# Fourteen modulation blocks: split fp32r products exchanged for plain fp32 products on four column groups

## What is computed

```python
mod = (jax.nn.silu(c) @ w_ada + b_ada)[:, None, :]
sh1, sc1, gt1, sh2, sc2, gt2 = jnp.split(mod, 6, axis=-1)
h = rmsnorm(x, g_mix) * (1 + sc1) + sh1
z = h @ w_in
...
x = x + gt1 * (merged @ w_out)
h2 = rmsnorm(x, g_ffn) * (1 + sc2) + sh2
```

## Time and profile before

| | |
|---|---|
| median of 3 runs | 1964.58 us (1964.14 to 1965.5) |
| profiled execution | 1967.0 us, of which the span from first to last instruction is 1965.3 us |
| TensorE busy | 1908.4 us (97%) |
| weight loads busy | 1815.0 us (92%), beside the matmuls |
| VectorE, ScalarE, GpSimd busy | 829.4 us (42%), 621.2 us (32%), 128.4 us (7%) |
| DMA | 257.70 MB, mean 131 GB/s |

### The profile page before, as it was taken

One profiled execution on the slowest core, in us unless ns is written; L12 is line 12 of the kernel. 1 busy time (PEld: TensorE's weight loads), 2 busy tenths in 40 slices (PEclk: granted clock), 3 DMA queues, 4 the chain that ended last, 5 costly groups with the idle time before them and its releaser, 6 DMA issues.

```text
span 1965.3 us, 30471 instructions
## 1 busy us (share of the span) xinstructions
PE 1908.4 (97%) x12193; PEld 1815.0 (92%) x12193; DVE 829.4 (42%) x1363; ACT 621.2 (32%) x952; POOL 128.4 (7%) x245
## 2 busy tenths in 40 slices
PE   7999999999999999999999997899999999999998
PEld 4799989999999997777899997899999999999998
DVE  5422222213334333232553558844455545564542
ACT  4331222222434433121210215533333334343432
POOL 0010009201000002221000000000000000000000
PEclk9999999999999999999999998999999999999999
DMA  8653434452343345544642350422232223774641
GB/s 273 239 177 120 132 122 135 140 151 73 93 128 106 92 150 129 165 142 143 203 123 89 90 175 25 109 67 67 71 111 80 65 65 119 261 240 149 214 152 63
DMA packets 254045, 257.70 MB, mean 131 GB/s; under 512 B 15476, under 2 KB 213160, under 8 KB 253952
## 3 DMA queue, kind: packets, MB, share of 16 engines
q1 hardware_dynamic: 244830, 222.81, 37.7%
q10 hardware_dynamic: 7721, 29.25, 3.7%
q0 software_dynamic: 1408, 4.46, 0.8%
HBM read 189.97 MB, written 66.63 MB: 131 GB/s over the span
## 4 chain that ended last, share of the span: by engine, by line
PE 92%; DVE 3%; ACT 2%; DMA 1%; issue 1%; SPq 0%; ACTq 0%; DVEq 0%
PE dense L2340 44%; PE dense L2760 17%; PE dense L2805 10%; PE misc L2760 5%; PE misc L2805 3%; PE misc L2641 2%; PE misc L2628 1%; PE misc L2567 1%; PE misc L2571 1%; PE misc L2540 1%; DMA ada_w<-in_w_ada_dram 1%; PE dense L2414 1%; PE misc L2569 1%; PE misc L2461 1%; PE misc L2460 1%
## 5 line engine op out<-in xcount | busy, mean ns | idle before, releaser
L2340 PE MATMUL dense<-act_hi,w_hi 128*128 128x384 f32 x1704 | 401.2, 343 | 5.8 <-DVE act_lo L1593 3.0
L2340 PE MATMUL dense<-act_lo,w_hi 128*128 128x384 f32 x1704 | 377.4, 329 | 0.0
L2340 PE MATMUL dense<-act_hi,w_lo 128*128 128x384 f32 x1704 | 376.9, 329 | 0.0
L2340 PEld LDWEIGHTS dense<-act_hi,w_hi 128*128 128x128 f32 x1704 | 291.9, 189 | 28.3 <-issue 21.4
L2340 PEld LDWEIGHTS dense<-act_hi,w_lo 128*128 128x128 f32 x1704 | 293.0, 189 | 0.0
L2340 PEld LDWEIGHTS dense<-act_lo,w_hi 128*128 128x128 f32 x1704 | 292.0, 189 | 0.0
L1588 DVE TENSOR_TENSOR w_lo<-raw,w_hi 128x1024 fp32r<-128x1024 f32 x73 | 92.4, 1267 | 265.9 <-ACT w_hi L1028 265.8
L1124 ACT ACTIVATE stage<-dense 128x768 f32<-128x768 f32 x52 | 42.2, 812 | 285.1 <-PE dense L2340 285.0
L1028 ACT ACTIVATE w_hi<-raw 128x1024 fp32r<-128x1024 f32 x73 | 77.3, 1060 | 167.7 <-PE dense L2340 167.3
L2047 DVE TENSOR_TENSOR w_lo<-hmT,w_hi 128x512 fp32r<-128x512 f32 x120 | 78.9, 686 | 101.2 <-ACT w_hi L1334 101.2
L1334 ACT ACTIVATE w_hi<-hmT 128x512 fp32r<-128x512 f32 x120 | 72.6, 623 | 81.2 <-PE dense L2760 80.8
(11 more groups left out here) (435 smaller groups left out, 3051.2 us busy)
## 6 DMA issues: line engine op xcount, KB each, us to landing
z_scratch<-stage ACTq DMA_DIRECT2D x52, 544.0 KB, 2.7
raw<-in_w_in_dram SPq DMA_DIRECT2D x53, 512.0 KB, 3.8
ada_w<-in_w_ada_dram SPq DMA_DIRECT2D x24, 1024.0 KB, 5.5
hmT<-in_w_gate_up_dram SPq DMA_DIRECT2D x40, 512.0 KB, 6.1
raw<-in_w_down_dram SPq DMA_DIRECT2D x34, 512.0 KB, 4.4
stage<-in_w_down_dram SPq DMA_DIRECT2D x32, 512.0 KB, 4.4
stage<-z_scratch SPq DMA_DIRECT2D x24, 544.0 KB, 3.7
a_scratch<-sums SPq DMA_DIRECT2D x34, 272.0 KB, 4.8
```

The source lines that it names most:

```text
L2340: ins = pe.matmul(tile(k, c), w[:, n % 2, off:off + P], x[:, xr, t0:t1], start=(first and p == 0), stop=(last and p == 2))
```

## The change

The late blocks are made as plain fp32 products. There are no high and low parts of the late `w_ada` blocks and of the condition any more; `c32` holds the condition in 32 columns (9 used, the rest zero). The 8 tiles of the contraction go in turn to four column groups of the array, each with 32 columns, so that each group adds up two tiles, and the four partial sums stand in PSUM rows 0, 32, 64 and 96 on. ScalarE copies all 128 rows. The turn is a product with a 0/1 matrix `pick` (128 x 9), which adds the four partial sums while it turns them. GpSimd makes `pick` from the identity. VectorE then has one operation per block. The blocks go into two slots of `ada_w` in turn, and a load waits until the modulation of the block two before is written (`mod_ready`).

```diff
         c32 = sb(halved, "c32", [P, KT, CW])
-                if per or j:
-                    sp.wait_ge(ada_cut, i * per + j)
+                if per or j > 1:
+                    sp.wait_ge(mod_ready, i * per + j - 1)
                 else:
-                    sp.wait_ge(mrow_ready, 7)
-                sp.dma_start(ada_w[:, 0, :, :], w_cols(...)
+                    sp.wait_ge(mrow_ready, (7, 10)[j])
+                sp.dma_start(ada_w[:, j % 2, :, :], w_cols(...)
...
+            pool.wait_ge(consts_ready, 3)
+            link(pool.tensor_tensor(pick[:, :], ident[:, 0:GRP], ident[:, CW:CW + GRP], ALU.add))
+            for j in range(2, P // CW):
+                link(pool.tensor_tensor(pick[:, :], pick[:, :], ident[:, CW * j:CW * j + GRP], ALU.add))
...
-            def ada_high(j, i=0):
-                act.activation(wa_hi[:, :, :], ada_w[:, 0, :, :], ACT.Copy).then_inc(adahi_ready, 1)
-            act.activation(c_hl[:, :, 0:GRP], cT[:, :, :], ACT.Copy).then_inc(chi_ready, 1)
-            ada_high(0)
+            act.activation(c32[:, :, 0:GRP], cT[:, :, :], ACT.Copy).then_inc(chi_ready, 1)
...
-                        act.activation(ada_rows[:, :], bank(r, 256, 2 * GRP), ACT.Copy).then_inc(round_free[r % 2], 1)
-                        if not last or j == 0:
-                            ada_high(1 + j // 2, i)
+                        act.activation(ada_rows[:, :], bank(r, 256), ACT.Copy).then_inc(round_free[r % 2], 1)
...
-                dve.tensor_tensor(wa_lo[:, :, :], ada_w[:, 0, :, :], wa_hi[:, :, :].bitcast(F32), ALU.subtract
-                                  ).then_inc(ada_cut, 1)
+            dve.memset(c32[:, :, GRP:CW], 0.0).then_inc(c_ready, 1)
...
-                    for col in range(2):
-                        ...
-                        ins = dve.tensor_scalar(out, t[:, 0:GRP], vec[:, ds(m + V_ADA, 1)], None, ALU.add)
-                        ...
-                        ins = dve.tensor_tensor(out, out, t[:, GRP:2 * GRP], ALU.add)
+                    dve.tensor_tensor(mod[:, ds(m, 2), :], bank(r, 2 * GRP).rearrange("p (m g) -> p m g", g=GRP),
+                                      vec[:, ds(m + V_ADA, 2)].unsqueeze(2).to_broadcast([P, 2, GRP]), ALU.add
+                                      ).then_inc(mod_ready, 1)
+                    dve.wait_ge(mod_ready, i + 1)
                     dve.sem_inc(round_free[r % 2], 1)
...
-                pe.wait_ge(ada_cut, i * (per // 2) + (jt // 2 + 1))
+                pe.wait_ge(ada_in[jt // 2], i * (per // 4 * 16) + 16)
-                for kk in range(KT):
-                    pe.matmul(bank(r, 256, 2 * GRP), c_hl[:, kk, :], wa_hi[:, kk, :], start=(kk == 0), stop=False)
-                    ins = pe.matmul(bank(r, 256, GRP), c_hl[:, kk, 0:GRP], wa_lo[:, kk, :], start=False,
-                                    stop=(kk == KT - 1))
+                for k0 in (0, KH):
+                    for j in range(KH):
+                        ins = pe.matmul(bank(r, 256)[CW * j:CW * j + CW, :], c32[:, k0 + j, :], ada_w[:, jt // 2, k0 + j, :],
+                                        start=(k0 == 0), stop=(k0 == KH))
...
-                    ins = pe.transpose(misc[:, r % 2, 2 * GRP * col:2 * GRP * (col + 1)],
-                                       ada_rows[:, P * col:P * col + P], ident[0:2 * GRP, 0:2 * GRP])
+                    ins = pe.matmul(misc[:, r % 2, GRP * col:GRP * col + GRP], ada_rows[:, P * col:P * col + P], pick[:, :],
+                                    start=True, stop=True)
...
                     pe.wait_ge(c_ready, 1)
+                    pe.wait_ge(consts_ready, 4)
```

More of the change, by code:

```diff
@@ L80 @@
 ADA0 = 20
+CW = 32
 ADA_EARLY = (0, 4, 1, 5, 2, 6, 3, 7, 8, 9)
@@ L130, in trunk @@
         epsc = sb(top, "epsc", [P, 1])
+        pick = sb(top, "pick", [P, GRP])
         raw = sb(top, "raw", [P, 2, 1024])
@@ L163, in trunk @@
         sb(halved, "over_x", [P, TT * D + KT * T + 600])
[L164 to L168, removed]
+        sb(halved, "over_ada_w2", [P, 2048])
+        c32 = sb(halved, "c32", [P, KT, CW])
+        ada_rows = sb(halved, "ada_rows", [P, 256])
         halved.close()
@@ L544, in late_ada_load @@
                 a = ADA0 // 2 + j
-                if per or j:
-                    sp.wait_ge(ada_cut, i * per + j)
-                else:
-                    sp.wait_ge(mrow_ready, 7)
-                sp.dma_start(ada_w[:, 0, :, :], w_cols(w_ada[0], i * (256 * per) + 256 * a, 256)
+                if per or j > 1:
+                    sp.wait_ge(mod_ready, i * per + j - 1)
+                else:
+                    sp.wait_ge(mrow_ready, (7, 10)[j])
+                sp.dma_start(ada_w[:, j % 2, :, :], w_cols(w_ada[0], i * (256 * per) + 256 * a, 256)
                              ).then_inc(ada_in[a % 2], 16)
@@ L1028, in split_hi @@
                 act.activation(w_hi[:, n % 2, :], raw[:, n % 2, :], ACT.Copy).then_inc(hi_ready, 1)
-            def ada_high(j, i=0):
-                wait_full(act, ada_in, j, i, 2, 16)
-                act.activation(wa_hi[:, :, :], ada_w[:, 0, :, :], ACT.Copy).then_inc(adahi_ready, 1)
             act.dma_start(cc[0:1, :], c_prompt).then_inc(c_in, 16)
@@ L1676, in _ @@
                 early_mod(e)
-            def ada_low(j, i=0):
-                dve.wait_ge(adahi_ready, i + (j + 1))
-                dve.tensor_tensor(wa_lo[:, :, :], ada_w[:, 0, :, :], wa_hi[:, :, :].bitcast(F32), ALU.subtract
-                                  ).then_inc(ada_cut, 1)
             dve.wait_ge(chi_ready, 1)
-            dve.tensor_tensor(c_hl[:, :, GRP:2 * GRP], cT[:, :, :], c_hl[:, :, 0:GRP].bitcast(F32), ALU.subtract
-                              ).then_inc(c_ready, 1)
-            ada_low(0)
+            dve.memset(c32[:, :, GRP:CW], 0.0).then_inc(c_ready, 1)
             split_lo(2)
@@ L1697, in body @@
                     if not last:
-                        ada_low(1, i)
                         split_lo(U_L1 + 3, i, 2)
                     wait_full(dve, round_full, r, i, 2)
-                    for col in range(2):
[L1702 to L1705, removed]
-                        ins = dve.tensor_scalar(out, t[:, 0:GRP], vec[:, ds(m + V_ADA, 1)], None, ALU.add)
-                        ins.then_inc(mod_ready, 1)
-                        dve.wait_ge(mod_ready, i * 4 + (2 * col + 1))
-                        ins = dve.tensor_tensor(out, out, t[:, GRP:2 * GRP], ALU.add)
-                        ins.then_inc(mod_ready, 1)
-                        dve.wait_ge(mod_ready, i * 4 + (2 * col + 2))
+                    m = i * 2 + ADA0
+                    dve.tensor_tensor(mod[:, ds(m, 2), :], bank(r, 2 * GRP).rearrange("p (m g) -> p m g", g=GRP),
+                                      vec[:, ds(m + V_ADA, 2)].unsqueeze(2).to_broadcast([P, 2, GRP]), ALU.add
+                                      ).then_inc(mod_ready, 1)
+                    dve.wait_ge(mod_ready, i + 1)
                     dve.sem_inc(round_free[r % 2], 1)
```

## The result

The changed kernel takes 1954.71 us (median of 5 runs, 1953.17 to 1955.3), the kernel before 1965.5 us beside it (5 runs, 1964.14 to 1966.55): a ratio of 0.9944, 95% interval 0.9929 to 0.9958, so 10.8 us or 0.6% less. The forecast was 1969.4, slower; what came is rival 1 (1954.2). The stated range, 1953 to 1972, holds the result only because it reached over both cases. The profiled execution took 1953.43 us, its span is 1951.7 us.

What follows compares the result with a forecast made beforehand. TensorE's own queue was taken as the bound: per late block 2.26 - 1.88 + 0.01 = +0.39 us, +5.5 over 14 blocks, less 0.7 for one wait, +4.8. Forecast 1969.4 us, slower, range 1953 to 1972.

Steps and rivals of the forecast that it cites:

- rival 1: Late blocks' products: four column groups run side by side, -0.69 us per block, 1954.2 us in all; chance 0.30, partly so included.
- 9 steps: Late product: one group's second half runs with the next group's first, nothing passes; 2.26 us against 1.88, chance 0.48.
- The bound: Late blocks, 88 to 456 us: TensorE's queue counts; removing VectorE's and ScalarE's parts, some 59 us, gains only at one wait.
- The changes of shape: Around each late product, array going narrow and back: 0.09 + 0.03 + 0.09 + 0.11 = 0.32 us per block.
- The step: Late product: instructions on the same columns start 0.2154 us apart, as read from the early blocks.
- The turn: After each late product: two full products in two halves each, 0.44 us against 0.43, +0.01 per block.
- The wait: TensorE before the pooling rows' transposes: 4.03 us shortens to 3.3, a gain of 0.7, kept at 0 to 2.3.
- The clock: After the pooling-row wait, granted at 0.57 over 4 us; a shorter gap escaping that might give up to 1.6 us more.
- The own range: Whole kernel if the likeliest case holds, varying 0.1 less or 0.15 more per block and the clock: 1966.4 to 1971.9 us.
- The moved loads: Late loads wait for an earlier modulation; a weight load moves from 304.59 to about 315 us, 5 us of cover left.
- The three prices: Late product at 16, 9 or 4 steps: 3.77, 2.26 or 1.18 us, against 1.88 before.
- 4-step case: Late product with four groups always side by side: 1.18 us against 1.88, 1954.2 us in all; chance 0.30, partly so included.

Runs made afterwards that it cites:

- The first experiment: Changed kernel with a late block's eight matmuls ordered by groups 0, 0, 1, 1, 2, 2, 3, 3 instead of 0, 1, 2, 3 twice: 1955.13 us, ratio 0.9948.
- How far ahead: Changed kernel with the late product issued group by group, each group's two matmuls made four times over: 2102.01 us, ratio 1.0689 to the kernel before.
- the double product: Changed kernel with the whole product of each late block made twice in a row: 1965.58 us, ratio 0.9999 to the kernel before.
- the cheap early products: Changed kernel with the ten early modulation blocks also made on four column groups and turned by the 0/1 product: 1948.64 us, ratio 0.9908 to the kernel before.

## Why the prediction was wrong

**The step that failed** is the choice of 9 steps: "if groups can run side by side but no matmul passes an earlier one (in all rows here matmuls start in program order)". The premise was read from rows in which every matmul uses the same columns as the one before, and there a column that is busy and an order that is kept look alike: the earlier trace rows could not tell them apart. I said so of the groups ("no row has two neighbours in the queue on different groups") but not of the order, which rests on the same rows. The first experiment shows halves starting past as many as nine earlier ones, and the experiment "How far ahead" that this goes as far as four halves of each group. The Trainium skill, page TensorE: Matmul & The Clock Gate (Part 3, The mechanism), says that matmuls are strictly first in, first out; the trace does not agree for fp32 matmuls on different column groups, and the measurement decides. With the rule of the Trainium skill's page TensorEngine Tiling (Key Properties), that tiles operate independently, the trace agrees: 16, 8 and 4 steps on one, two and four groups. It agrees only as far as no group has more than two matmuls in line, as the experiment "How far ahead" shows.

That one term is 14 x (2.26 - 1.19) = 15.0 us, and the forecast and the result lie 14.7 us apart. The rest of the sum, point by point:
- **The bound.** Right: 39 us of VectorE's and 20 us of ScalarE's work fell away in the stretch of the late blocks, and TensorE's rhythm moved by TensorE's own part alone.
- **The changes of shape**, 0.32 us per visit, put together from the column sums: 0.33 by the double product, which takes them as one. By the raw starts around block 0 the single terms were near too: 0.08 us on the way in, 0.02 on the first step, 0.12 on the way out and 0.10 for the full load, where 0.09, 0.03, 0.09 and 0.11 were forecast.
- **The step** of 0.2154 us holds on each group; 3.77, 2.26 and 1.18 us were the prices of 16, 9 and 4 steps, and 1.19 was measured for the 4.
- **The turn**: 0.44 us forecast, 0.44 measured.
- **The wait**: 0.7 less forecast, 1.16 measured. The step "with the same hand-over about 0.5 us" was too long for one operation (0.28), and 0.2 us came from ahead of VectorE. The clock did not escape: after the shorter wait it is granted at 0.57 again, as in the earlier trace rows.
```profile
286.00:290.00 4.00, 4.00 (x18) 4.00 (x17) 0.76 (x2) 0.00 (x0) 2.83 (x3) 0.57 0.81 256
```
- **The own range** of the 9-step case: its upper end, 1971.9, is 0.3 too low, since 0.15 us on 14 blocks and the 0.7 of the wait make 2.8 on 1969.4. Nothing hangs on it.
- **The moved loads**: hidden, as forecast. Block 7's modulation came at 285.33, the load that waited for it at 285.66, and the weight load behind it at 308.39 rather than the forecast 315. TensorE has two waits of over 1 us from 85 to 456 us and none for the weights' low part (who, for whom: us, times, longest):
```profile
PE misc L2508 <- DVEq L1693: 2.9, 1, 2.9
PE misc L2522 <- DMA qkv<-z_scratch: 2.5, 1, 2.5
```
The second of them stands in the kernel before too, with 2.1 us.

The three prices were right, and the chances were not: 0.30 for the case that came. An even weight on the 9-step and the 4-step case was what the rows bore out, since nothing in them spoke on the order across groups.

## What to carry to other kernels

A narrow fp32 product of which the result needs few columns can be spread over column groups by splitting its contraction: its time is then the halves of the fullest group times a step, plus about a third of a microsecond for each visit to the narrow shape. In this shape, keep no more than two fp32 matmuls in line per group before the other groups' come, or deal them out in turn. And before a cheaper product is put in elsewhere, read which engine bounds that stretch, and the granted clock in the profile after: here the same edit was worth 2.5 us a block behind VectorE's rounds, next to nothing beside them, and ahead of them the lower clock took most of it back.

## What the runs showed of the hardware

- Matmuls on different column groups start 6.7 ns apart when dealt out in turn and 13.4 ns apart when they have to pass others; four then run together, and none of the product's instructions starts for the next 0.2 us.
- Matmuls of one group start 0.216 us apart (256 columns, plain fp32, each matmul two halves), whether one, two or four groups are at work.
- A half of another group passes what waits as long as no group has more than four halves, under way or waiting, in front of it; a fifth holds up everything behind it (52 steps where 16 halves of each group stood in line).
- With the cheap early products, where TensorE waited for loads and for ScalarE's copies of the rows, the granted clock was 0.50 from 23 to 33 us and 0.74 from 34.0 to 66.5 us, against 1.00 in the changed kernel for both. VectorE's rounds hid what the second cost; the first made six matmuls in the chain take 3.96 us where they had taken 2.02.
